# Attention maxima by pairs of matmuls on 64 rows each, from the high part of q; their broadcast by four matmuls with a repeated column

## What is computed

```python
def one_block(qblk):
    s = jnp.einsum('bqkgd,bskd->bkgqs', qblk, k, preferred_element_type=jnp.float32)
    p = jax.nn.softmax(s.astype(jnp.float32), axis=-1).astype(v.dtype)
    return jnp.einsum('bkgqs,bskd->bqkgd', p, v)
```

## Time and profile before

| | us |
|---|---|
| median of 3 runs | 1740.67 |
| lowest and highest | 1738.71, 1743.01 |
| the profiled execution's own time | 1742.83 |
| its span, first to last instruction | 1741.0 |
| TensorE busy | 1617.9 (93%) |
| VectorE busy | 1015.4 (58%) |
| ScalarE busy | 815.8 (47%) |
| POOL busy | 500.0 (29%) |

### The profile page before, as it was taken

How to read it: one execution, slowest core, us unless ns; L and a number is a source line. 1 busy time by engine, 2 the same in 40 slices (tenths; PEclk the granted TensorE clock), 3 DMA queues, 4 the chain that set the end, 5 groups by cost and what they waited for, 6 DMA issues and landing times. The chain is left out here.

```text
span 1741.0 us, 21425 instructions
## 1 busy us (share of the span) xinstructions
PE 1617.9 (93%) x7112; PEld 1275.0 (73%) x7112; DVE 1015.4 (58%) x1476; ACT 815.8 (47%) x1021; POOL 500.0 (29%) x275
## 2 busy tenths in 40 slices
PE   7698894899999999999999999997999997999998
PEld 1387784577777777777777777776888885977886
DVE  0367876678778778778777787753000160255452
ACT  1455442276766666666766766661111021242111
POOL 0033332144544545445545545441000000000000
PEclk9699997699999999999999999998999997899999
DMA  6655542600000000000000000009323113168661
GB/s 212 252 182 162 186 145 81 197 22 24 15 21 15 24 21 15 25 22 16 24 21 15 21 24 15 21 6 275 110 86 116 49 47 156 60 165 201 189 183 73
DMA packets 113798, 152.20 MB, mean 87 GB/s; under 512 B 15665, under 2 KB 78129, under 8 KB 113362
## 3 DMA queue, kind: packets, MB, share of 16 engines
q1 hardware_dynamic: 107074, 138.92, 25.3%
q0 software_dynamic: 6672, 12.58, 2.4%
HBM read 105.21 MB, written 46.27 MB: 87 GB/s over the span
## 5 line engine op out<-in xcount | busy, mean ns | idle before, releaser
L826 DVE TENSOR_REDUCE chunk_max<-max_ps 128x1 f32<-128x512 f32 (+1 forms) x640 | 395.7, 635 | 68.4 <-PE max_ps L892 63.0
L755 POOL TENSOR_TENSOR prob_lo<-prob,prob_hi 128x1024 fp32r<-128x1024 f32 x128 | 307.0, 2398 | 419.2 <-ACT prob L788 419.2
L787 ACT ACTIVATE prob_hi<-s_ps 128x1024 fp32r<-128x1024 f32 x288 | 295.2, 1025 | 231.3 <-PE s_ps L910 231.2
L788 ACT ACTIVATE prob<-s_ps 128x1024 f32<-128x1024 f32 x288 | 293.5, 1019 | 0.0
L892 PE MATMUL max_ps<-k_hi,blk_q_hilo 128*128 128x512 f32 (+1 forms) x640 | 248.2, 390 | 31.1 <-DVE chunk_max L826 18.2
L909 PE MATMUL s_ps<-blk_q_hilo,k_hi 128*128 128x512 f32 x576 | 233.1, 405 | 1.1 <-DVE blk_q_negm L842 0.8
L930 PE MATMUL hi_ps<-prob_hi,v_hl 128*128 128x512 f32 x576 | 228.2, 396 | 1.4 <-POOL prob_lo L755 0.9
L910 PE MATMUL s_ps<-blk_q_negm,k_lo 65*128 65x512 f32 x576 | 229.2, 398 | 0.0
L932 PE MATMUL lo_ps<-prob_lo,v_one 128*128 128x512 f32 x576 | 229.0, 398 | 0.0
L931 PE MATMUL lo_ps<-prob_hi,zero_one 128*128 128x512 f32 x576 | 227.4, 395 | 0.0
L848 DVE TENSOR_TENSOR prob_lo<-prob,prob_hi 128x1024 fp32r<-128x1024 f32 x160 | 197.1, 1232 | 28.6 <-ACT prob L788 28.6
(11 more groups left out here) (209 smaller groups left out, 2358.9 us busy)
## 6 DMA issues: line engine op xcount, KB each, us to landing
w_mod<-in_w_mod SPq DMA_DIRECT2D x6, 2048.0 KB, 17.5
x<-in_x SPq DMA_DIRECT2D x8, 1024.0 KB, 5.4
h_scratch<-h_hi SPq DMA_DIRECT2D x8, 1024.0 KB, 4.2
h_scratch<-h_lo SPq DMA_DIRECT2D x8, 1024.0 KB, 6.6
q_scratch<-q_hilo SPq DMA_DIRECT2D x16, 512.0 KB, 3.2
blk_q_hilo<-q_scratch SPq DMA_DIRECT2D x32, 256.0 KB, 2.8
hh<-h_scratch SPq DMA_DIRECT2D x4, 2048.0 KB, 10.8
hl<-h_scratch SPq DMA_DIRECT2D x4, 2048.0 KB, 15.5
```

The source lines that it names most:

```text
L755: nc.gpsimd.tensor_tensor(prob_lo[slot3(j)][:], prob[slot3(j)][:], prob_hi[slot3(j)][:].bitcast(F32), ALU.subtract).then_inc(s_lo_pool, 1)
L787: nc.scalar.activation(prob_hi[slot3(j)][:], s[:], ACT.Exp)
L788: nc.scalar.activation(prob[slot3(j)][:], s[:], ACT.Exp).then_inc(s_exp, 1)
L826: last = nc.vector.reduce_max(chunk_max[:, qt, kc:kc + 1], bank[:, 0:MAX_CHUNKS[kc]], X_AXIS)
```

## The change

- The maxima are taken from the high part of q alone. A pair of uses is issued together: the first takes its weights from rows 0 to 63 of `q_negm` and its keys from rows 0 to 63 of `k_hi2`, the second its weights from rows 64 to 127 of a new buffer `q_dup` (the high part of q again) and its keys from rows 64 to 127 of `k_hi2`. They write the two banks. The two of a pair have the same keys and two query tiles (`max_unit`). Ahead of a pair TensorE waits until both banks are free.
- `MAX_AT` counts pairs: 1, 2, 2, 2, 2, 1 in passes 0 to 5. A pair stands behind scores e = 0 and a second one behind values e = 0.
- VectorE reduces both uses of a pair, then the next; its low part stands behind the first pair of a pass.
- POOL makes the low parts of passes 0, 2, 3, 4, 5 and 6 in place of 0, 2, 4 and 6.
- The diagonal products go. The broadcast is four matmuls of 128 columns, whose weights are one column of `neg_max` repeated and whose moving operand is the identity, rounded once ahead of the loop (`ident_r`).
- SP loads `q_dup` for each block, a third DMA of 128 KB.

```diff
-MAX_AT = (4, 4, 3, 4, 3, 2, 0, 0, 0)
-LO_AFTER = (2, 0, 1, 0, 1, 0, 0, 0, 0)
+MAX_AT = (1, 2, 2, 2, 2, 1, 0, 0, 0)
 MAX_ROW_AT = 6
 PAIRS = KT // 2
-POOL_LO = (0, 2, 4, 6)
+POOL_LO = (0, 2, 3, 4, 5, 6)
+
+
+def max_unit(u):
+
+    pair, i = divmod(u, 2)
+    group, chunk = divmod(pair, len(MAX_CHUNKS))
+    return 2 * group + i, chunk
...
         q_negm = [sb(f"blk_q_negm{i}", [P, QB], F32R) for i in range(2)]
+        q_dup = [sb(f"blk_q_dup{i}", [P, QB], F32R) for i in range(2)]
         chunk_max = sb("chunk_max", [P, QB // P, len(MAX_CHUNKS)])
-        neg_max = sb("neg_max", [P, QB // P])
-        diag = sb("diag", [P, QB], F32R)
+        neg_max = sb("neg_max", [P, QB // P], F32R)
+        ident_r = sb("ident_r", [P, P], F32R)
...
                 sp.dma_start(q_negm[slot][0:HD, :].bitcast(F32), q_v[b][0:HD, :]).then_inc(s_q[slot], 16)
+                sp.dma_start(q_dup[slot][HD:P, :].bitcast(F32), q_v[b][0:HD, :]).then_inc(s_q[slot], 16)
...
                 nc.vector.tensor_reduce(neg_max[:], chunk_max[:], X_AXIS, ALU.max, negate=True).then_inc(s_neg, 1)
-                dve.wait_ge(s_neg, b + 1)
-                for qt in range(QB // P):
-                    last = nc.vector.tensor_scalar(diag[:, qt * P:(qt + 1) * P], k.ident[:], neg_max[:, qt:qt + 1],
-                                                   None, ALU.mult)
-                last.then_inc(s_diag, 1)
...
+            nc.vector.tensor_copy(ident_r[:], k.ident[:]).then_inc(s_ident, 1)
             for u in range(MAX_USES):
                 reduce(0, 0, u)
...
                         if n < n_max:
                             reduce(b + 1, 1 - slot, u)
-                            u += 1
-                        if n == min(LO_AFTER[j], max(n_max, 1) - 1) and j + 1 < PAIRS:
+                            reduce(b + 1, 1 - slot, u + 1)
+                            u += 2
+                        if n == 0 and j + 1 < PAIRS:
                             lo(b, slot, j + 1)
...
             def max_use(b, slot, kvh, u):
-                qt, kc = divmod(u, len(MAX_CHUNKS))
-                bank = max_ps[(slot * (MAX_USES + 1) + u) % 2]
                 if u == 0:
-                    pe.wait_ge(s_q[slot], (b - slot) * 16 + 32)
-                pe.wait_ge(s_mfree, b * (MAX_USES + 1) + (u + 1))
-                key0 = sum(MAX_CHUNKS[:kc])
-                nc.tensor.matmul(bank[:, 0:MAX_CHUNKS[kc]], q_hilo[slot][:, qt * P:(qt + 1) * P],
-                                 k.k_hi2[:, kvh, key0:key0 + MAX_CHUNKS[kc]], start=True, stop=True).then_inc(s_mfull, 1)
+                    pe.wait_ge(s_q[slot], (b - slot) * 24 + 48)
+                pe.wait_ge(s_mfree, b * (MAX_USES + 1) + (u + 2))
+                for i, q in enumerate((q_negm[slot], q_dup[slot])):
+                    qt, kc = max_unit(u + i)
+                    bank = max_ps[(slot * (MAX_USES + 1) + u + i) % 2]
+                    key0 = sum(MAX_CHUNKS[:kc])
+                    rows = slice(i * HD, (i + 1) * HD)
+                    nc.tensor.matmul(bank[:, 0:MAX_CHUNKS[kc]], q[rows, qt * P:(qt + 1) * P],
+                                     k.k_hi2[rows, kvh, key0:key0 + MAX_CHUNKS[kc]], start=True,
+                                     stop=True).then_inc(s_mfull, 1)
 
             def broadcast_max(b, slot):
-                pe.wait_ge(s_diag, b + 1)
+                pe.wait_ge(s_neg, b + 1)
                 pe.wait_ge(s_mfree, b * (MAX_USES + 1) + (MAX_USES + 1))
                 bank = max_ps[(slot * (MAX_USES + 1) + MAX_USES) % 2]
-                nc.tensor.matmul(bank[:], k.ones_sq[:], diag[:], start=True, stop=True).then_inc(s_mfull, 1)
+                for qt in range(QB // P):
+                    last = nc.tensor.matmul(bank[:, qt * P:(qt + 1) * P], neg_max[:, qt:qt + 1].broadcast_to([P, P]),
+                                            ident_r[:], start=True, stop=True)
+                last.then_inc(s_mfull, 1)
...
                         f(*args)
-                        if n < n_max:
+                        if n % 2 == 0 and n // 2 < n_max:
                             max_use(b + 1, 1 - slot, next_kvh, u)
-                            u += 1
+                            u += 2
```

More of the change, by code:

```diff
@@ L688, in attention @@
         s_vone = S("v_one_ready")
-        s_neg, s_diag = S("neg_max_done"), S("diag_ready")
+        s_neg, s_ident = S("neg_max_done"), S("ident_rounded")
         s_score, s_exp = S("scores_ready"), S("scores_exponentiated")
@@ L821, in reduce @@
             def reduce(b, slot, u):
-                qt, kc = divmod(u, len(MAX_CHUNKS))
+                qt, kc = max_unit(u)
                 bank = max_ps[(slot * (MAX_USES + 1) + u) % 2]
@@ L840, in max_row @@
                 dve.wait_ge(s_mfull, b * (MAX_USES + 1) + (MAX_USES + 1))
-                dve.wait_ge(s_q[slot], (b - slot) * 16 + 32)
+                dve.wait_ge(s_q[slot], (b - slot) * 24 + 48)
                 nc.vector.tensor_copy(q_negm[slot][HD:HD + 1, :], bank[HD:HD + 1, :]).then_inc(s_mfree, 1)
@@ L934, in pv @@
                     last.then_inc(s_pv, 1)
-            for u in range(MAX_USES):
+            for u in range(0, MAX_USES, 2):
                 max_use(0, 0, 0, u)
             pe.wait_ge(s_vone, 1)
+            pe.wait_ge(s_ident, 1)
             broadcast_max(0, 0)
```

## The result

| | before | after |
|---|---|---|
| median of 4 runs, us | 1740.87 | 1798.72 |
| lowest to highest | 1738.71 to 1743.01 | 1796.33 to 1801.35 |
| profiled span, us | 1741.0 | 1796.3 |

The ratio is 1.0333 (95% interval 1.0313 to 1.0352): 3.3% slower, 58 us. The forecast was 1785 us.

What follows compares the result with a forecast made beforehand. TensorE was taken to bound the kernel. Profiled 1742.8 us + 39 for the blocks + 5.6 for the start = 1787.4, less 2.2 from profiled run to median: 1785 us, range 1760 to 1828.

Steps and rivals of the forecast that it cites:

- The ring: Maxima pairs: pair, its two reductions, then the next pair; 1.96 us against TensorE's 1.40, a 0.56 us wait per wide pair.
- (a): Ten pairs replace twenty maxima matmuls: the second of a pair is free, saving some 2.1 us per block.
- (b): Wait for both banks before a pair: 1.96 us from pair to pair; block sum +1.26 us, +39 us over 31 blocks.
- (f): Array shape changes around each pair: bounded by 0 or 0.17 us on each side, taken as 0; the least certain term.
- (c): Broadcast by four 128-column matmuls: 0.40 us in place of 0.23, counted in the block sum; diagonal products gone gain nothing.
- (d): Low parts of passes 3 and 5 on POOL: nothing waits, though part 2 has only 0.1 us to spare.
- (e): Start ahead of the loop, at half clock: slower pairs, fewer diagonal products, a third load; together +5.6 us.
- rival that the array empties: Array drains at every change of shape around the pairs: 1804 us in place of 1785; chance 0.24 with the former rival's 1811.
- rival of hidden weights: Weights of a waiting pair are loaded ahead after all: pair to pair 1.86 us, about 1765 us; chance 0.08.
- halves in line: Rival: the two matmuls of a pair run one after the other, +7 us, 1792 us; chance 0.18.
- pairs keep pace: Rival, passes 1 to 4: pairs follow at 1.40 us for the full gain and the kernel is faster, 1653 us; chance 0.04.
- TensorE's busy share falls: Sign in the profile: TensorE's busy share drops from 93% to below 90%.

Runs made afterwards that it cites:

- e1: Changed kernel, but each maxima reduction reads only the first half of its bank and the exponentials are scaled to stay finite; 1776.8 us.
- e5: e1 with both matmuls of a pair in rows 0 to 63, so that they can't run at once; 1843.1 us.
- e2: Changed kernel with its pairs on all 128 rows: no change of array shape, the wait for both banks kept; 1781.4 us.
- e3: Changed kernel with the edits of e1 and e2 together: short reductions and pairs on all 128 rows; 1724.9 us.
- e6: Kernel before with the new broadcast alone: four matmuls of 128 columns, no diagonal products; 1742.6 us, ratio 1.0007.
- e7: Kernel before with only the low parts of passes 3 and 5 moved to POOL; 1741.3 us, ratio 1.0004.
- e4: Kernel before with each of the 20 single maxima matmuls of a block reading rows 0 to 63 only; 1963.0 us.

## Why the prediction was right or wrong

The direction held, 1798.7 lies in the range, and the forecast was 14 us short. The mechanism held in part. The ring is there and sets the pace at wide pairs, but by 0.08 us and not by the 0.56 forecast. The prediction had the ring as the only cost: without it a kernel faster than before should be left, and e1 measures 1777. The changes of shape, put at nothing, are the second limit, nearly as long as the ring.

- (a) *Two at once, one slot*: right, 66 us by e5.
- (b) *The ring*: right in kind, too long in size: 1.96 forecast, 1.88 measured. The step that was off is "two reductions 1.38": back to back on full banks they take 1.29. The earlier trace rows had it already: the two reductions from 601.85, of 512 and 256 columns, take 1.02, where the prices of the earlier trace rows add up to 1.11. In e2, where the ring acts alone, it costs 56.5 us against e3.
- (f) *The change of array shape, "I take 0"*: **the step that failed.** I bounded it by 0.17 on each side, which was near, and then took nothing; the pair pays 0.09 ahead, 0.10 for its own weights, 0.10 behind and 0.10 for the next weights, 0.39 in all. I had not thought of the weights: they are not loaded ahead across a change of shape. The Trainium skill ("TensorEngine Tiling (Array Packing)", Key Properties) says that a change of tiling mode drains the array. The 0.09 ahead of the pair and the 0.10 behind it agree with that, though no run parts a drain from the weight load.
- These two errors met. TensorE's own part is 1.79 and not 1.40, so the stall at a pair is 0.08 us, not 0.56, and the time went where I did not look: pair 1 at 3.50 (laid out: 3.04), pair 5 at 10.81 (10.53). Pair 9 then came at 18.31 (18.27): that is luck, a late first pair made good by shorter rings. The block ended at 28.20, not 27.75. Of the 0.45 that is missing, 0.19 is the way out of pair 9 and 0.20 the wait of pass 7 for the row of maxima. The laid-out block leaves that wait out, while the measured block of before, from which it is taken off, has it: 0.20 x 31, some 6 us of the 14, have nothing to do with ring or shape.
- (c) *Broadcast*: the price was right (0.40). In the kernel before it hides in the wait of pass 7 (e6); in the changed kernel 0.14 of the 0.17 is paid.
- (d) *Low parts*: right, nothing (e7).
- (e) *The start*: +5.6 forecast; the first score matmul comes at 328.93 in place of 323.53, 5.4 later. Two small errors meet in it: the first pair goes out 1.1 us later (0.6 forecast), and the wide ring there is 2.17 (2.25).
- The rival that the array empties (1804) was nearest. Its sum charged only the exits and entries that no stall hides; the rows have a cost at every pair, most of it under the ring. The ring of 1.88 is close to the 1.86 of the rival of hidden weights, but by faster reductions: the weights of a waiting pair are not hidden. The halves in line are out (e5); that the pairs keep pace is out twice over, since e1 lifts the ring and stays at 1777.
- Of the signs: couples together, seven waits a block and clock 1.00 came true, and so did the gap at a couple that waits for nothing (pair 0). The length of the waits told nothing: 0.45 on average, as forecast, at a loss of 0.08. "TensorE's busy share falls" was wrong, it stayed at 93% and rose within the attention.

## What to carry to other kernels

Work in half the array saves one slot and pays for the way in and out: one pair between full-array matmuls saved 0.21 us and cost 0.39. Since the price is per change (e5), more pairs behind one another should earn it back; no run here tried that. Taking two buffers at once turns double buffering into a ring of fill and drain; its length is to be laid against the producer's own work, with the prices of the consumer when its input is ready. A length of waits in the profile is no measure of loss; start-to-start slots are. Where two limits are this close, removing one shows little; take away each alone and both together before naming the cause.

## What was not expected of the hardware

- A matmul on 64 rows among those on 128 costs 0.38 to 0.39 us more, one on 65 rows nothing (e4).
- A weight load takes 0.19 us. In a stream of one shape it starts a slot (0.23 us) ahead and costs nothing; across a change of shape it starts with its own matmul and shows as durations of 0.49 to 0.50 in place of 0.39 to 0.40, of the pair and of the matmul behind it.
- In e4 the granted clock stayed at 0.50 from 330 to 366 us while TensorE was shown busy without a gap.
- A reduction of 512 columns takes 0.69 us by itself and 0.60 from start to start when the next bank is already full.
